# Starting the GEMM behind each adaLN norm on rows that are not yet normed

## The reference

```python
def rms_norm(x, g):
    y = xf * lax.rsqrt(jnp.mean(xf * xf, axis=-1, keepdims=True) + EPS)
    return (y * g).astype(x.dtype)
def modulate(x, m, i):
    return x * (1 + scale_i) + shift_i          # both from the condition, per feature
def ffn_sublayer(x, m, i, g, w_in, w_out):
    u = modulate(rms_norm(x, g), m, i)
    a, b = jnp.split(u @ w_in, 2, axis=-1)
    return (jax.nn.silu(a) * b) @ w_out
# one block: x += gate_0/2 * ffn(0); x += gate_1/2 * mixer(1) (its q, k, f, v, gates read the same u);
#            x += gate_2/2 * ffn(2)            (512 tokens: 256 of context, 256 latent)
```

## Time and profile before

| | us |
|---|---|
| three runs | 2753.29, 2754.08, 2756.24 (median 2754.08) |
| the profiled execution | 2759.6 |
| its span, first to last instruction | 2757.8 |
| mean granted TensorE clock over the span | 0.978 |

### The profile page before, as it was taken

One profiled execution on the slowest core, in us unless ns is written; L12 is line 12 of the kernel. 1 busy time (PEld: TensorE's weight loads), 2 busy tenths in 40 slices (PEclk: granted clock), 3 DMA queues, 4 the chain that ended last, 5 costly groups with the idle time before them and its releaser, 6 DMA issues.

```text
span 2757.8 us, 42480 instructions
## 1 busy us (share of the span) xinstructions
PE 2634.6 (96%) x15112; PEld 2268.3 (82%) x15112; DVE 1395.3 (51%) x3037; ACT 1023.9 (37%) x1747; POOL 1312.6 (48%) x654
## 2 busy tenths in 40 slices
PE   7998989979999999999999999999999999998997
PEld 7968989978888878867787888878888878887997
DVE  3562765675544442355497444454455453647222
ACT  4345457442322132166513232232321232463542
POOL 4505858744443434133343444444443453455875
PEclk9999989989999999999999999999999999999999
DMA  5604635554443443121243443444443453324554
GB/s 191 222 24 154 213 121 184 176 159 153 148 136 112 125 148 122 39 85 46 77 148 128 144 144 113 120 130 156 137 132 115 148 169 100 100 93 138 168 164 124
DMA packets 413994, 365.71 MB, mean 133 GB/s; under 512 B 7484, under 2 KB 412558, under 8 KB 413888
## 3 DMA queue, kind: packets, MB, share of 16 engines
q1 hardware_dynamic: 411448, 359.14, 41.0%
q10 hardware_dynamic: 2440, 5.16, 0.5%
HBM read 363.19 MB, written 1.08 MB: 132 GB/s over the span
## 4 chain that ended last, share of the span: by engine, by line
PE 68%; issue 14%; POOL 12%; DVE 3%; ACT 2%; DMA 0%; POOLq 0%; SPq 0%; ACTq 0%; DVEq 0%
PE bank L1615 57%; POOL w_lo L655 12%; PE bank L2021 2%; PE bank L1675 1%; PE bank L1676 1%; PE bank L1680 1%; PE bank L2061 1%; PE bank L1625 1%; PE bank L1966 1%; DVE stat L1521 1%; PE bank L1767 1%; PE bank L1958 1%; PE bank L2047 0%; PE bank L1978 0%; DVE bank L1145 0%
## 5 line engine op out<-in xcount | busy, mean ns | idle before, releaser
L655 POOL TENSOR_TENSOR w_lo<-raw,w_hi 128x1024 fp32r<-128x1024 f32 (+2 forms) x602 | 1285.9, 2150 | 1343.9 <-ACT w_hi L726 936.2
L1615 PE MATMUL bank<-u_hi,w_hi 128*128 128x512 f32 (+1 forms) x2488 | 854.0, 343 | 2.8 <-POOL w_lo L655 2.8
L1615 PE MATMUL bank<-u_hi,w_lo 128*128 128x512 f32 (+1 forms) x2488 | 845.9, 340 | 0.0
L1615 PE MATMUL bank<-u_lo,w_hi 128*128 128x512 f32 (+1 forms) x2488 | 845.2, 340 | 0.0
L726 ACT ACTIVATE w_hi<-raw 128x1024 fp32r<-128x1024 f32 (+3 forms) x412 | 387.0, 954 | 985.7 <-PE bank L1615 794.3
L1615 PEld LDWEIGHTS bank<-u_hi,w_hi 128*128 128x128 f32 x2488 | 473.5, 190 | 74.8 <-issue 25.1
L1615 PEld LDWEIGHTS bank<-u_hi,w_lo 128*128 128x128 f32 x2488 | 473.6, 190 | 52.7
L1615 PEld LDWEIGHTS bank<-u_lo,w_hi 128*128 128x128 f32 x2488 | 473.7, 190 | 49.1
L1189 DVE SCALAR_TENSOR_TENSOR bank<-mod_raw,cond,bank 128x256 f32<-128x256 f32 x864 | 344.7, 481 | 1.4 <-DMA mod_raw<-in_w_mod 1.4
L1615 PE MATMUL bank<-hid_hi,w_hi 128*128 128x512 f32 (+1 forms) x880 | 309.8, 352 | 11.3 <-POOL w_lo L655 11.3
L1615 PE MATMUL bank<-hid_hi,w_lo 128*128 128x512 f32 (+1 forms) x880 | 307.0, 349 | 0.0
(11 more groups left out here) (239 smaller groups left out, 3387.2 us busy)
## 6 DMA issues: line engine op xcount, KB each, us to landing
raw<-in_ffn_w_in SPq DMA_DIRECT2D x88, 1024.0 KB, 5.1
mod_raw<-in_w_mod SPq DMA_DIRECT2D x144, 512.0 KB, 4.3
raw<-in_w_in SPq DMA_DIRECT2D x67, 1024.0 KB, 5.2
raw<-in_ffn_w_out SPq DMA_DIRECT2D x64, 704.0 KB, 4.6
raw<-in_w_ffn_up SPq DMA_DIRECT2D x22, 1024.0 KB, 5.1
raw<-in_w_ffn_down SPq DMA_DIRECT2D x16, 704.0 KB, 4.8
raw<-in_w_attn_out SPq DMA_DIRECT2D x8, 1024.0 KB, 5.2
raw<-in_w_o SPq DMA_DIRECT2D x8, 1024.0 KB, 5.2
```

The lines of the kernel that those rows point to most:

```text
L655: pool.tensor_tensor(st.half(t, w_lo[slot]), st.half(t, raw[slot]), st.half(t, w_hi[slot]).bitcast(f32), ALU.subtract).then_inc(lo_ready, 1)
L1615: ins = pe.matmul(dst, s, v, start=first and n == 0, stop=final and n == 2)
```

## The change

For each of the six norms, the first two weight blocks of the GEMM behind it ("late blocks") now multiply u_hi and u_lo of x * a, without root and shift. Those values are made while the GEMM before still runs: ACT writes the rounded part of a finished tile of `x` (`early_tiles`), DVE the rest (`early_rest`). For W.shift, PE multiplies the two late blocks with a 4-column operand (`shift_parts`: two token kinds, hi and lo; 32 matmuls for each block, `shifts`). The sums of squares and the spread stand between the k steps of the first late block. When a late block is done, ACT copies its banks to `work` or `q2`, DVE multiplies by the root (`scale`), ACT adds the shift (`finish`). The normed u is then written over the early one, tile by tile as the second late block leaves it. At n1_1 it is written in 16 passes of one half each, the latent half first.

Along with it: the last square is added to `root` too, which leaves one operand for the sums. The modulation pairs are placed anew: none in the first body of a GEMM that begins with late blocks, none in w_o, q_1 and f_1; two to a body in down_00, down_01 (and so none left for others), one more in the gates. `modulation(l, 2)` is made ahead of w_o and no longer between its two bodies. For n0_0 the context half is made early ahead of the last body of down1, the latent half inside `norm_x`.

```diff
+            def early_rest(at, i, halves):
+
+                for h in halves:
+                    cols = slice(h * S, (h + 1) * S)
+                    by = mod_a[:, i, at, h:h + 1] if isinstance(at, int) else mod_a[:, i, at, h]
+                    ins = dve.scalar_tensor_tensor(u_lo[:, at, cols], x[:, at, cols], by, u_hi[:, at, cols].bitcast(f32),
+                                                   ALU.mult, ALU.subtract)
+                ins.then_inc(early_lo, 1)
...
+            def late_norm(name, st, late_tile):
...
+                def take_shift():
+                    dve.wait_ge(shift_done, plan.at(name, "shift") + st.n_late)
...
+                dve.reciprocal(rms[:, 1, 0:nt], rms[:, 0, 0:nt]).then_inc(diag_ready, 1)
+                take_shift()
+                dve.wait_ge(bcast_done, plan.at(name, "bc") + 1)
+                if st.n_late == 2:
+                    scale(0)
+                    scale(1)
+                for n in range(len(passes) + 1):
+                    if n < len(passes):
+                        norm(n)
+                    if n >= 1:
+                        rest(n - 1)
...
+                dve.wait_ge(u_ready, u0 + len(passes))
+                if st.n_late == 2:
+                    scale(2)
+                    scale(3)
...
+                def first(st):
+                    late_norm(st.late, st, late_work(w))
+                    dve.wait_ge(hid_ready, base + 1)
+                    for t in range(2):
+                        tile(st, 0, t, late_halves(st.late) if st.n_late == 2 else None)
...
-                        sum_squares(st, i, t, x[:, bass.ds(i * tiles + t, 1), span(halves)], S * len(halves),
-                                    final)
+                        sum_squares(st, i, t, x[:, at, span(halves)], S * len(halves), final)
+                        if nxt is not None:
+                            dve.wait_ge(early_hi, i * tiles_per + (plan.at(nxt, "early") + t + 1))
+                            early_rest(at, int(nxt[1]), late_halves(nxt))
...
+                    if st.n_late == 2:
+                        for t in range(2):
+                            split_half(st, 0, t)
+                            take(st, t)
+                        for t in range(2):
+                            finish(t)
+                        for n in range(len(passes)):
+                            hi(st, n)
+                            if n == KD - 1:
+                                for t in range(2):
+                                    split_half(st, 1, t)
+                                    take(st, 2 + t)
+                        if func == ACT.Identity:
+                            for t in range(2, 4):
+                                finish(t)
...
+            def shifts(name, st, l, c):
...
+                    for k in range(KD):
+                        w = slice(k * BLK + t * P, k * BLK + (t + 1) * P)
+                        for n, part in enumerate((w_hi[slot], w_lo[slot])):
+                            ins = pe.matmul(bank[2][:, at:at + 4], part[:, w], shift_parts[:, k, :],
+                                            start=k == 0 and n == 0, stop=k == KD - 1 and n == 1)
...
+            def norm_beside(name, w):
+
+                def after(c, k):
+                    if (c, k) == (0, 5):
+                        shifts(name, [st for st in stream if st.late == name][0], int(name[3]), 1)
+                    if (c, k) == (0, 0):
+                        column_sums(name, w)
+                    if (c, k) == (0, 1 if w == T else 2):
+                        spread(name, w)
...
-                column_sums(f"n1_{l}", T)
-                spread(f"n1_{l}", T)
-                gemm(f"q_{l}", features(*u_of(span(q_h)), wq), u_tile(f"n1_{l}"))
+                shifts(n1, gemms[f"q_{l}"], l, 0)
+                gemm(f"q_{l}", features(*u_of(span(q_h)), wq), u_tile(n1),
+                     late=late_blocks(n1, span(q_h), wq, claim_tile, norm_beside(n1, T)))
```

More of the change, by code:

```diff
@@ L241, in make_plan @@
         plan.add(f"att_{l}", b3=units, unit=units, o=KD)
[L242 to L245, removed]
+        gemm(f"attn_out_{l}", cols(a["w_attn_out_2"][l], 0), 4, mod=0 if last else 1, counted=False)
+        gemm(f"w_o_{l}", cols(a["w_o_2"][l], 0), 4, acc=4, whole=True)
+        first = late_norm(f"n2_{l}", 2, halves=halves)
+        gemm(f"up_{l}1", pairs(a["ffn_w_in_2"][l, 1]), 22, mod=0 if last else 1, mod_bodies=range(1, 11),
+             banks=(0, 1), **first)
         gemm(f"down_{l}1", down(a["ffn_w_out_2"][l, 1]), 16, per=4, kt=DOWN_KT, cols=P, banks=(0, 1),
-             mod=not last, acc=2)
+             mod=0 if last else 2, acc=2, whole=not last)
     norm("n_final", TO_OUT, summed=True)
@@ L467, in two_blocks @@
         block = ctx.enter_context(nc.Block())
+        LATE = {st.late for st in stream if st.late is not None}
         SCORE1 = (0, 1, 6)
@@ L812, in silu_tiles, with late_rows, evac @@
+            def late_rows(dst, cols):
+                def evac(st, t):
+                    act.wait_ge(group_done, st.done(0, t + 1))
+                    act.activation(dst[:, t, cols], bank[t][:, 0:cols.stop - cols.start], ACT.Copy).then_inc(taken[t], 1)
+                return evac
             def silu_tiles(w, base):
@@ L1123, in norm_x @@
                 for k in range(KD):
+                    if then is not None and k >= 1:
+                        then(k - 1)
                     g = col[:, COL[gain] + k:COL[gain] + k + 1]
@@ L1447, in ffn @@
-                gemm(name, body)
-            def residual(i_mod, halves, per, tiles):
-                def body(st, i, final):
-                    for t in range(tiles):
+                        tile(st, i, t)
+                def first(st):
+                    late_norm(st.late, st, late_work(w))
+                    dve.wait_ge(hid_ready, base + 1)
+                    for t in range(2):
+                        tile(st, 0, t, late_halves(st.late) if st.n_late == 2 else None)
+                gemm(name, body, first=first)
@@ new lines, in residual, with early_context, early_latent @@
+                return body
+            def early_context():
+                modulation(0, 0)
+                for k in range(KD):
+                    dve.wait_ge(early_hi, plan.at("n0_0", "early") + k + 1)
+                    early_rest(k, 0, [CTX])
+            def early_latent(k):
+                dve.wait_ge(early_hi, plan.at("n0_0", "early") + KD + k + 1)
+                early_rest(k, 0, [LAT])
+            clear_sums()
+            gemm("down1", copy_y(2, 4), between=early_context)
+            norm_x("n_ffn_post", "g_ffn_post", then=early_latent)
```

521 lines of the change are left out of this document (374 added, 147 removed).

## The result

| | before | after |
|---|---|---|
| runs, median us | 2753.91 (2753.29 to 2756.24, 4 runs) | 2800.48 (2797.44 to 2809.53, 4 runs) |
| profiled execution | 2759.6 | 2801.53 |
| its span | 2757.8 | 2799.7 |
| mean granted clock | 0.978 | 0.974 |

The ratio is 1.0172, 95% interval 1.0157 to 1.0188: 46.6 us slower, 41.9 between the two profiled executions. Forecast were 2792 and a loss of 38. The profiled execution lies 5.7 us above the median in the kernel before, and 1.1 above it in the changed one.

What follows compares the result with a forecast made beforehand. PE was taken as the bound, busy 2634.6 of 2757.8 us; 4.5 + 10.5 + 0 + 8 + 10 + 5 = +38 gave 2797.6 profiled, median 2792, own range 2772 to 2812, stated range 2746 to 2818.

Steps and rivals of the forecast that it cites:

- W.shift: At all six norms, 384 added four-column matmuls on PE at 0.115 us each, 7.4 us a norm, 44 in all.
- no difference: Rival: W.shift's weight loads hide and a matmul costs 0.04 us, giving 2750 to 2763; chance 0.11.
- The idle time that the late blocks fill is thus handed to W.shift: At n1_0, n2_0, n0_1: a stretch of 32.0 us against 31.0 less 0.9, +1.5 each on average, +4.5.
- Hidden tile: Behind the up GEMMs of n0_0, n2_0, n0_1: PE waits 3.5 us each for bank 2, +10.5.
- Wide norms: At n1_0, n2_0, n0_1: new stretch of 32.0 us against 31.0 less 0.9, +4.5 in all.
- n0_0: At n0_0: 20 us of usable waiting, but PE's transposes come 0 to 5 us later; 0, between -8 and +5.
- n1_1: At n1_1: the second body of q_1 waits 8.3 us for bank 2; +6 to +12, taken +8.
- n2_1: At n2_1: DVE's last square comes late, PE waits for it, then for bank 2; +9 to +15, taken +10.
- Clock: At the wide norms: W.shift stretches may let the granted clock fall, +5 in all (0 to 25).
- much slower: Rival: the clock falls in each of the twelve light stretches, about +40 on the forecast, 2830; chance 0.10.

Runs made afterwards that it cites:

- e4: The changed kernel with W.shift taken over only the first of eight k tiles, 48 four-column matmuls instead of 384: 2773.17 us, ratio 1.0064 to the kernel before.
- e9: The changed kernel with scaled tiles 2 and 3 written into their banks in the up stages, so the late product has one SBUF operand: 2792.06 us, ratio 1.0129.
- e1: The changed kernel with the former norm restored at all six norms, the moved modulation pairs kept: 2755.45 us, ratio 1.0000 to the kernel before.
- e2: The changed kernel with only n0_0 late and the other five norms as before: 2763.69 us, ratio 1.0028 to the kernel before.
- e6: The changed kernel with ACT's eight early context tiles in down1 put behind the first split of the last body: 2802.32 us, ratio 1.0165.
- e5: The changed kernel with q tiles 2 and 3 at n1_1 finished after two of the eight context passes: 2796.68 us, ratio 1.0147.
- e10: The changed kernel with W.shift in free columns of bank 4 instead of bank 2 at all norms but n0_0: 2795.78 us, ratio 1.0149.

## Why the prediction was right, and where its terms were off

The time lies in the forecast's own range (2772 to 2812), 8.5 us above its point, and by the forecast's mechanism. Of the 8.5 us only 3.9 lie between the forecast 2797.6 and the measured 2801.53 of the profiled execution. The other 4.5 come from taking for granted that it would lie 5.5 above the median again; it lay 1.1 above. By its steps:

- **W.shift, 0.115 us a matmul, 44 us.** Measured 0.109 at full clock, 42. The rival "no difference", which needed 0.04, falls with that. e4 shows how much of it was on the path: 27 us came off, and 13.9 returned as DVE's lag. The step "The idle time that the late blocks fill is thus handed to W.shift" holds.
- **Hidden tile, +3.5 at three places, +10.5.** Measured 2.78, 2.62 and 2.72, so 8.1, and 2.02 more at n2_1, where 4 to 6 were expected. The cause was named as a possible price, two SBUF operands beside POOL; e9 makes it the cause of the greater part (6.2 of the 10.1 at all four).
- **Wide norms.** Forecast 4.5, two hidden tiles 7.0 and clock 5: 16.5. Measured 18.8 over e1. The 4.5 is itself added up a little low: its own terms, 32.0 against 31.0 less 0.9, give 1.9 a norm and 5.7.
- **n0_0, 0, with the hidden tile 3.5.** Measured 5.0 in the profiled execution, 8.2 in e2's median. The late context tiles of down1 were seen as DVE's delay of PE's transposes. That did not come: DVE's products for the modulation start at 571.07, earlier than the 576.22 of the earlier trace rows even with the 3.2 us by which this execution is ahead. It was ACT: it stands waiting for `modulation` with four weight splits queued behind, which by e6 is 3.1 of down1's 6.0. The prediction's sentence on that step left out what is queued behind the waiting instruction on ACT.
- **n1_1, +8.** The wait for bank 2 was forecast with 8.3 us and measured with 8.23, and e5 shows the queue order as its cause. The stage costs 12.7 over e1 and 11.4 over the kernel before; 6.8 of it is clock by the estimate above, where the prediction let the low clock give 2.3 back and 3 more.
- **n2_1, +10.** 8.8 with w_o_1. The lag of DVE is there (its last sum ends 12.2 us behind the last matmul of w_o_1, where 13.4 were forecast; rows below, two squares and sums at several times their usual 0.43 beside POOL), but PE meets it at bank 2, ahead of W.shift, and not at the sums. e10 moves it to the sums, as forecast there.

```profile
2561.62 0.28 PE L1885 MATMUL bank<-m_hi,w_lo 128*128 128x256 f32 x1
```

```profile
2559.77 2.39 DVE L1393 TENSOR_TENSOR xn<-x 128x256 f32<-128x256 f32 x1
2562.20 2.44 DVE L1398 TENSOR_TENSOR root<-root,xn 128x256 f32<-128x256 f32 x1
...
2567.43 2.33 DVE L1393 TENSOR_TENSOR xn<-x 128x256 f32<-128x256 f32 x1
2569.79 2.46 DVE L1398 TENSOR_TENSOR root<-root,xn 128x256 f32<-128x256 f32 x1
...
2573.66 0.42 DVE L1398 TENSOR_TENSOR root<-root,xn 128x256 f32<-128x256 f32 x1
```

```profile
2559.47 4.88 POOL L716 TENSOR_TENSOR w_lo<-raw,w_hi 128x1024 fp32r<-128x1024 f32 x2 [4.09 <-ACT w_hi L776]
2567.12 4.85 POOL L716 TENSOR_TENSOR w_lo<-raw,w_hi 128x1024 fp32r<-128x1024 f32 x2 [2.76 <-ACT w_hi L776]
```

- **Clock, +5 at the wide norms.** By the estimate it takes 5.0 us there, n0_0 included. What was mis-sized is the clock at the narrow norms: 12.4 us, where the prediction had some 3 to 4 within each. Over all norms that is 17.4. No run changes the clock alone, so this share stays an estimate. It lies between the forecast and the rival "much slower", whose rule (every one of the twelve stretches low) is refuted: of the twelve, two ran at 0.21 us a matmul, two at 0.13 and 0.14, and eight at 0.109 to 0.117 (each from the first and the last start of its 32). The clock is low also over dense matmuls behind such a stretch, as at 2586.4 to 2589.8 us:

```profile
2248.50:2255.30 6.80, 6.80 (x33) 6.80 (x34) 0.72 (x3) 1.85 (x3) 0.72 (x1) 0.51 0.00 0
...
2586.40:2589.80 3.40, 3.40 (x18) 3.40 (x18) 0.60 (x2) 2.76 (x5) 1.62 (x1) 0.52 0.00 0
```

PE is busy for the whole of both stretches of the changed kernel and has half the clock. The first begins within W.shift of the second late block (2246.05 to 2250.5) and goes on over dense matmuls, the second begins 1.4 us behind it.

## What to carry to other kernels

Filling a wait with work that has to be done anyway gains only what the wait is worth less what the split of the work adds; here 9 us stood against 7 of W.shift at each wide norm, and the chains behind it and the clock did the rest. A matmul with 128 stationary columns and 4 moving ones takes 0.109 us, one with 4 stationary and 256 moving 0.116 and does the work of two; so of two operands the small one should be the stationary one. Before a chain on another engine is shortened at its start, look in its rows for an instruction that takes several times its usual duration: that one, not the number of steps, was the greater part of the hidden tile's wait.

## What the runs showed of the hardware

- 32 matmuls with a stationary operand of 128 columns and 4 moving ones take 3.5 us; the same products as 16 matmuls with 4 stationary columns and 256 moving ones take 1.85, and the granted clock is low for half as much of PE's busy time (45.0 us against 87.6).
- In the changed kernel the clock at one norm differs from execution to execution though its instructions are the same: at n1_0 PE is busy at 0.50 for 10.2, 0 and 6.8 us in the traces of the changed kernel, e5 and e6, and the stage is 4.2 and 1.6 us shorter than in the first, about half of the difference. So the time of one stage in one execution is only good to some 4 us here; medians over runs, or the busy time at either clock, are needed to judge an edit of that size.
- An instruction of DVE that takes 0.44 us took 2.5 (half of 4.93) beside POOL, with two operands in SBUF; with one of them in PSUM it took 0.44 again.
